# Cached keys turned in 32x32 blocks on VectorE, and logits on 32x32 TensorE tiles

## What is computed

```python
def moba_sample(q, k_new, v_new, cache_k, cache_v, page_table, slopes):
    ...
    k_past = cache_k[page_table].reshape(DB, past, H, D)
    ...
    k_mean = jnp.mean(kb.astype(jnp.float32), axis=2)
    ...
    idx, valid = moba_select(qh, q_pos, k_mean)
    ...
    o = moba_attend(qh, q_pos, k_sel, v_sel, idx, valid, k_own, v_own, ob * MOBA_BLOCK, slopes)

def trunk_layer(x, hist, start_pos, attend, norm1_g, w_in, w_pool, pool_scale, w_out, norm2_g, w_gate, w_up, w_down):
    h = rmsnorm(x, norm1_g)
    z = h @ w_in
    q, k, v, u = jnp.split(z, [ATTN_WIDTH, 2 * ATTN_WIDTH, 3 * ATTN_WIDTH], axis=-1)
    ...
    a = attend(q, k, v)
    p, new_hist = pool_mixer(u, hist, start_pos, w_pool, pool_scale)
    x = x + jnp.concatenate([a, p.astype(a.dtype)], axis=-1) @ w_out
    h2 = rmsnorm(x, norm2_g)
    x = x + (jax.nn.silu(h2 @ w_gate) * (h2 @ w_up)) @ w_down
```

## Time and profile before

| what | value |
|---|---|
| time, median of 3 runs | 1643.3 us (1643.12 to 1644.52) |
| the profiled execution | 1645.28 us |
| its span in the trace | 1643.3 us |
| PE busy | 1570.4 us, 96% |
| DVE, ACT, POOL busy | 759.0, 600.8, 104.1 us |
| read from HBM, mean rate | 328.10 MB, 203 GB/s |
| cached-attention phase | 81.5 to 581.5 us |

### The profile page before, as it was taken

How to read it: one execution, slowest core, us unless ns; L and a number is a source line. 1 busy time by engine, 2 the same in 40 slices (tenths; PEclk the granted TensorE clock), 3 DMA queues, 4 the chain that set the end, 5 groups by cost and what they waited for, 6 DMA issues and landing times.

```text
span 1643.3 us, 33559 instructions
## 1 busy us (share of the span) xinstructions
PE 1570.4 (96%) x12884; PEld 1400.6 (85%) x12884; DVE 759.0 (46%) x1202; ACT 600.8 (37%) x874; POOL 104.1 (6%) x184
## 2 busy tenths in 40 slices
PE   6999999999999978899999999999999999999987
PEld 5976676666666657799999999999999999999986
DVE  4533233133133133556555555454545555555545
ACT  4333233332333333335433333333333434333333
POOL 3004151000000010002000000000000000000003
PEclk9998999999999987999999999999999999999998
DMA  5667988989889744745545455555555454544531
GB/s 194 224 202 254 336 306 292 341 283 326 320 308 322 269 132 153 225 165 160 164 167 166 166 158 168 163 163 164 166 166 166 155 171 162 164 165 155 177 128 58
DMA packets 154368, 333.80 MB, mean 203 GB/s; under 512 B 10464, under 2 KB 44313, under 8 KB 153728
## 3 DMA queue, kind: packets, MB, share of 16 engines
q1 hardware_dynamic: 154311, 333.05, 60.4%
HBM read 328.10 MB, written 5.27 MB: 203 GB/s over the span
## 4 chain that ended last, share of the span: by engine, by line
PE 93%; DVE 3%; ACT 2%; issue 1%; DMA 1%; SPq 0%; POOL 0%; DVEq 0%; POOLq 0%; ACTq 0%
PE bank L1185 24%; PE bank L1187 23%; PE bank L1186 23%; PE bank L1191 10%; PE bank L1295 6%; PE bank L1267 4%; PE bank L1328 1%; ACT kT L483 1%; DMA vec<-in_pool_scale 1%; PE bank L1361 1%; PE bank L1434 0%; DVE w_lo L709 0%; DVE d L793 0%; PE bank L1421 0%; ACT px L609 0%
## 5 line engine op out<-in xcount | busy, mean ns | idle before, releaser
L1185 PE MATMUL bank<-hh,w_hi 128*128 128x288 f32 x2176 | 654.8, 301 | 11.7 <-DVE xT L886 6.6
L1186 PE MATMUL bank<-hl,w_hi 128*128 128x288 f32 x2176 | 644.0, 296 | 0.0
L1187 PE MATMUL bank<-hh,w_lo 128*128 128x288 f32 x2176 | 642.2, 295 | 0.0
L709 DVE TENSOR_TENSOR w_lo<-w_raw,w_hi 128x1024 fp32r<-128x1024 f32 (+1 forms) x376 | 443.3, 1184 | 406.9 <-ACT w_hi L483 403.8
L483 ACT ACTIVATE w_hi<-w_raw 128x1024 fp32r<-128x1024 f32 x312 | 328.3, 1058 | 510.9 <-PE bank L1187 508.8
L1185 PEld LDWEIGHTS bank<-hh,w_hi 128*128 128x128 f32 x2176 | 410.1, 188 | 27.2 <-issue 17.0
L1187 PEld LDWEIGHTS bank<-hh,w_lo 128*128 128x128 f32 x2176 | 411.7, 189 | 0.0
L1186 PEld LDWEIGHTS bank<-hl,w_hi 128*128 128x128 f32 x2176 | 410.9, 189 | 0.1
L483 ACT ACTIVATE kT<-bank 128x512 f32<-128x512 f32 x256 | 149.4, 597 | 278.6 <-PE bank L1191 278.3
L1185 PE MATMUL bank<-ah,w_hi 128*128 128x288 f32 x704 | 210.0, 298 | 9.5 <-DVE af L1041 5.4
L1187 PE MATMUL bank<-ah,w_lo 128*128 128x288 f32 x704 | 210.1, 298 | 0.0
(11 more groups left out here) (176 smaller groups left out, 679.6 us busy)
## 6 DMA issues: line engine op xcount, KB each, us to landing
kpage<-in_cache_k SPq DMA_DIRECT2D x128, 512.0 KB, 5.6
vpage<-in_cache_v SPq DMA_DIRECT2D x128, 512.0 KB, 5.0
w_raw<-in_w_gate SPq DMA_DIRECT2D x88, 512.0 KB, 3.5
w_raw<-in_w_up SPq DMA_DIRECT2D x88, 512.0 KB, 3.5
w_raw<-in_w_down SPq DMA_DIRECT2D x88, 512.0 KB, 3.5
w_raw<-in_w_in SPq DMA_DIRECT2D x64, 384.0 KB, 6.6
w_raw<-in_w_out SPq DMA_DIRECT2D x32, 512.0 KB, 4.8
w_raw<-in_w_in SPq DMA_DIRECT2D x16, 512.0 KB, 4.2
```

The lines of the kernel that those rows point to most:

```text
L709: V.tensor_tensor(w_lo[:, s, 0:width], w_raw[:, s, 0:width], w_hi[:, s, 0:width].bitcast(F32), ALU.subtract).then_inc(lo_ready, 1)
L1185: PE.matmul(o, wh, xh[:, c, :], start=start and i == 0, stop=False)
L1186: PE.matmul(o, wh, xl[:, c, :], start=False, stop=False)
L1187: last = PE.matmul(o, wl, xh[:, c, :], start=False, stop=stop and i == len(chunks) - 1)
```

## The change

K pages are no longer turned by PE. DVE turns each page in place, in blocks of 32x32 (`turn_k`, one 128x1024 instruction for a page, four for a quad). A logit is a sum over 4 blocks of 32 of the head's 128 dimensions. These four sums accumulate in PSUM, and the 32 keys in a block lie in the free dimension, so that a matmul has 32 rows (32 key rows of a page, after the turn 32 dimensions), 32 stationary columns and 256 moving columns (4 pages, 2 heads, 32 keys). The 16 matmuls for one block of 32 dimensions go to the 16 tiles of 32x32 of the array. Both heads of a pair have their queries in the stationary block, and the half that belongs to the other head is dropped later by `pick`. For this, q is replicated to all row groups once (`replicate_q`, 4 matmuls; `qrep`) and spread with zeros into `qr` for each sequence (`pad_q`). The logits lie in four banks (`S`, 2 to 5) in another order, so `scaled_logits` is one reduce over 1024 columns, eight operations of 128x128 and four small ones; before it was one operation and one reduce of 128x512, and a small one. The copies to `kT` on ACT are gone.

Weight tiles of this phase are 512x256 (24 matmuls, 48 tiles, 4 for each block of 256 columns, in two banks), all within the first six of the eight steps. ACT makes `w_hi` of them, and DVE computes `w_lo` in place of `w_raw`; raw slots are 6 instead of 4 and wait for `w_used` of the tile six before. K is loaded two quads ahead and waits for `qk_done` of the quad two before, the first two K quads wait for nothing, each K page has a semaphore of its own, and the order on SP in a quad is two tiles, K, V. The steps are written out, without the loop. The running maxima and sums of a sequence stay on all partitions (`ml_sp`) and are brought to 32 by one matmul after the last step.

```diff
-            def load_k(i, j, free=True):
-                if free:
-
-                    sp.wait_ge(kt_in, 32 * i + 8 * j - 8)
+            def load_k(i, j):
+                n = NQUADS * i + j
+                if n >= 2:
+
+                    sp.wait_ge(qk_done, n - 1)
                 for g in range(4):
...
+            load_k(0, 0)
+            load_k(0, 1)
+            for i in range(NB):
                 for j in range(NQUADS):
-                    for k in (2 * j, 2 * j + 1):
...
+                    if i < KVU_STEPS:
+                        load_kvu(8 * i + 2 * j)
+                        load_kvu(8 * i + 2 * j + 1)
+                    ahead = NQUADS * i + j + 2
+                    if ahead < NQUADS * NB:
+                        load_k(ahead // NQUADS, ahead % NQUADS)
+                    if i:
+                        load_v(i - 1, j)
...
             def load(t, src, free=True):
 
-                n, _, s = t
+                n, _, s, _ = t
                 if free:
-                    sp.wait_ge(lo_ready, n - 3)
+                    sp.wait_ge(w_used, n - RAW + 1)
...
+            def turn_k(i, j):
+                n = NQUADS * i + j
+                for g in range(4):
+                    dve.wait_ge(k_in[n % 2][g], 16 * (n // 2) + 16)
+                    V.transpose(kpage[:, n % 2, g, :], kpage[:, n % 2, g, :]).then_inc(k_turned, 1)
+
+            def scaled_logits(b):
+                dve.wait_ge(qk_done, NQUADS * b + NQUADS)
...
+                own.did(V.tensor_reduce(d4[:, :, :].rearrange("p a u -> p (a u)"),
+                                        S.rearrange("p a (s k) -> p s a k", s=4), AX.XY, ALU.add))
+                for e in range(2):
+                    for a in range(4):
+                        keys = slice(32 * a, 32 * a + 32)
+                        own.did(V.scalar_tensor_tensor(ss[:, :, keys],
+                                                       S[:, a, P * e:P * e + P].rearrange("p (n i) -> p n i", n=4),
+                                                       pick[:, e:e + 1], (past_bias, ss)[e][:, :, keys],
+                                                       ALU.mult, ALU.add))
...
+            pad_q(0)
+            turn_k(0, 0)
+            for i in range(NB):
+                lo_kvu(i, 0)
+                if i:
+                    select_blocks(i - 1)
+                    joint_max(i - 1)
+                turn_k(i, 1)
...
+                lo_kvu(i, 3)
+                if i < NB - 1:
+                    scaled_logits(i)
+                    pad_q(i + 1)
+                    turn_k(i + 1, 0)
...
-                def logits(j, h):
...
-                    for g in range(4):
-                        last = PE.matmul(S[32 * g:32 * g + 32, P * j:P * j + P], qz[:, 32 * h:32 * h + 32],
-                                         kT[:, h % 2, P * g:P * g + P], start=h == 0, stop=h == H - 1)
-                    last.then_inc(qk_done, 1)
...
+            def logits(b, j):
+                n = NQUADS * b + j
+                pe.wait_ge(k_turned, 4 * n + 4)
...
+                for c in range(4):
+                    for a in range(4):
+                        for x in range(4):
+                            at_ = STRIP * (4 * c + x) + PAD - j
+                            keys = kpage[32 * a:32 * a + 32, n % 2, :, :].rearrange(
+                                "p n (e x c i) -> p e x c n i", e=2, x=4, c=4)[:, :, x, c, :, :]
+                            last = PE.matmul(S[32 * x:32 * x + 32, a, :], qr[32 * a:32 * a + 32, at_:at_ + 32], keys,
+                                             start=j == 0 and c == 0, stop=j == NQUADS - 1 and c == 3)
+                last.then_inc(qk_done, 1)
...
+            replicate_q()
+            for i in range(NB):
+                logits(i, 0)
+                if i:
+                    block_sums(i - 1)
+                if i >= 2:
+                    combine(i - 2)
...
+                for j in range(1, NQUADS):
+                    logits(i, j)
+                    if i:
+                        values(i - 1, j - 1)
+                    if i < KVU_STEPS:
+                        kvu_tile(8 * i + 2 * j)
+                        kvu_tile(8 * i + 2 * j + 1)
+                if i:
+                    values(i - 1, NQUADS - 1)
```

More of the change, by code:

```diff
@@ L152, in step_program @@
         hl = sb("hl", [P, KC, T], F32R)
-        w_raw = sb("w_raw", [P, SLOTS, TE])
-        w_hi = sb("w_hi", [P, SLOTS, TE], F32R)
-        w_lo = sb("w_lo", [P, SLOTS, TE], F32R)
+        w_hi = sb("w_hi", [P, HI, TE], F32R)
+        raw = ExitStack()
+        w_raw = sb("w_raw", [P, RAW, TE], stack=raw)
+        raw.close()
+        w_lo = sb("w_lo", [P, RAW, TE], F32R)
         gains = sb("gains", [P, 56])
@@ L203, in step_program @@
         pre.close()
+        kv_a.close()
         post = ExitStack()
@@ L237, in step_program @@
         late.close()
[L239 to L242, removed]
+        banks = ctx.enter_context(nc.psum_tensor("banks", [P, 8, 512], F32))
+        bank = [banks[:, n, :] for n in range(8)]
+        WB = bank[0:2]
+        S = banks[:, 2:6, 0:2 * P]
         OB = bank[6:8]
@@ L400, in _, with load_v @@
[L400 to L407, removed]
+                    sp.dma_start(kpage[:, n % 2, g, :], page(ck, i, 4 * j + g)).then_inc(k_in[n % 2][g], 16)
+            def load_v(i, j):
+                n = NQUADS * i + j
+                if n:
+                    sp.wait_ge(v_done, n)
+                else:
+                    sp.wait_ge(xT_in, KC)
+                    sp.wait_ge(hist_T, 2)
+                for g in range(4):
+                    sp.dma_start(vpage[:, g, :], page(cv, i, 4 * j + g)).then_inc(v_in, 16)
@@ L798, in select_blocks @@
-            def select_blocks(i):
-                dve.wait_ge(bs_done, i)
+            own.did(V.tensor_scalar(pick[:, :], pair, SCALE, None, ALU.mult))
+            own.link(V.memset(qr[:, :], 0.0))
+            dve.wait_ge(sq_added, KC)
+            V.tensor_copy(rep_w, ident.rearrange("p (c i) -> p c i", c=4).unsqueeze(2).to_broadcast([P, 4, 4, 32])
+                          ).then_inc(rep_table, 1)
+            dve.wait_ge(rep_in, 1)
+            for x in range(2):
+                V.tensor_copy(qrep[:, 16 * x:16 * x + 16, :],
+                              OB[x].rearrange("p (s t) -> p s t", t=TS)).then_inc(rep_taken, 1)
@@ L988, in _ @@
             add_pool_half(15)
-            for k in range(2, SLOTS):
-                lo(tile_at(T_OA + k))
             dve.wait_ge(wo_taken, KC)
@@ L998, in add_group @@
                     ins.then_inc(quad_taken[quad], 1)
-            for k in range(4, 20):
+            for k in range(2, 20):
                 lo(tile_at(T_OA + k))
@@ L1182, in w_tile @@
                         a = width * i + P * m
[L1183 removed]
+                        wh, wl = w_hi[:, u, a:a + P], w_lo[:, s, a:a + P]
                         o = out[:, 0:T]
@@ L1383, in _ @@
             mixer(1)
-            p_turned(NB, True)
+            p_turned(NB - 1)
+            pe.wait_ge(l_saved, NB)
+            PE.matmul(OB[1][0:32, 16:32], tb("first"), ml_sp[:, :, :].rearrange("p a b -> p (a b)"), start=True,
+                      stop=True).then_inc(ml_in, 1)
             for r in range(2, 8):
```

466 lines of the change are left out of this document (219 added, 247 removed).

## The result

The changed kernel takes 1664.6 us (median of 4 runs, 1662.73 to 1665.54) against 1643.2 us for the kernel before: a ratio of 1.013, 95% interval 1.0113 to 1.0148. It is 21 us slower, where 1623 us, 20 us faster, was forecast.

The account below looks back on a forecast made before the run. PE was taken as the bound, transfers close behind. Start 11, step 0 48, steps 1 to 5 300, steps 6 and 7 110, clock 8: 477 against 500; +3 later, so 1623 us, own range 1600 to 1650, 8 in 10 1580 to 1690.

Parts of the forecast that it names:

- The price of the logits: PE, logits of a quad: 64 added matmuls with all 16 tiles overlapping, 2.0 us a quad.
- Rival 4: PE's logits: row tiles take turns, 6.9 us a quad, about 1672 us; chance 0.08.
- The turns: DVE, turning K pages: 128 turns of 128x1024 at 1.2 us each, 4.8 a quad.
- Rival 3: DVE's turns take two passes, 2.46 us each, about 1680 us; chance 0.13.
- I take 12.8: Steady quad with V and tiles: two loops and the transfers all sit at 12 to 13 us; 12.8 taken.
- The loop of the tiles: Steady quads: K and V issue, tile issue, landing, split, tiles and values to next logits but one, 26 us for two quads.
- the 8 us that were set aside for the clock: Whole phase: PE pauses more often and its clock falls in some steps, 8 us added.
- The border: Between sequences, steps 1 to 5: DVE work makes 16.6 instead of 12.8 us to next logits; +9 in all with thin queue.
- their 55 us: Steps 6 and 7, without tiles: 13 us a quad through the single V buffer, 3 at the border, 55 each.
- The start: From the z copies to the first logits: pick, table and q copies, PE 1.4, four turns, some 11 us.
- Rival 2: Phase's transfers thin throughout, slower than before, at 267 GB/s for over half the bytes: about 1665 us; chance 0.15.
- Rival 1: Phase's transfer queue never runs dry, 151 MB at 414 GB/s: about 1580 to 1600 us; chance 0.17.

Follow-up runs that it names:

- the mended order: Changed kernel with SP issuing the next quad's tiles, then V, then K: 1615.3 us; with the start filled and last values behind the next logits too, 1589.8 us.
- the junk: Junk matmuls on PE between logits and values in steps 6 and 7: ten in the changed kernel, 1665.1 us; eight in the fastest (1589.8 us), 1595.6 us.

## Why the prediction was wrong

The direction was wrong, and by the steps it was this:

- **What bounds before** was read rightly: PE. Its relief was real (112 us less busy time), and PE was indeed no longer last.
- **The price of the logits** was too low, 2.0 against 2.68 us. In the first pass the instructions of the 16 tiles start 7 ns apart, but a pass of the sixteen takes 0.335 us on average (2.68 over 8) instead of 0.215. By the Trainium skill, "TensorE: Matmul & The Clock Gate", Part 3, the estimate was 2.6, and the trace agrees with the page. On PE, which has slack, 0.7 us a quad matter little, but SP issues K pages only when the logits are done, so they lie on the loop below. Rival 4 (6.9) is excluded.
- **The turns** were right, 1.213 us. Rival 3 is excluded; the estimate of 2.5 us, from the Trainium skill's "VectorE: DVE Perf Modes", The three transpose paths, is twice what an fp32 page of 128x1024 takes, and the measurement decides. The four turns do stand right ahead of the logits of a sequence's second quad (13.4 us in most steps), but the run with quarter turns shows that shortening them moves the time to the quads behind.
- **The step that failed is "I take 12.8"** for a steady quad. The quads inside steps 1 to 5 took 14.4 us on average, which is 4.8 of the 5.5 us that a step took beyond the 60. The loop of the tiles, reckoned at 26 us for two quads, took 30.5 to 31.6. Its sum names the logits but has no term for them: they took 2.7. The values, 1.9 in the sum, aren't in series. Issue and landing were put at 15.6 us and took 17.5 in the quad of step 2: the landing of 6.6 us came from the kernel before, with tiles of 384 KB and a median of four transfers in flight at their issue; now it was 7.7 to 10.0 with five to seven in flight in the loops that were read. The two tiles took 8.1 us instead of 6.4, at the lower clock for part of the time. That last item is of the size of the 8 us that were set aside for the clock: 1.7 us in each such loop, and one of them stands in each of steps 2 to 5.
- **The border** of steps 1 to 5 was nearly right in size and wrong in mechanism. The forecast had 12.8 + 9 = 21.8 us for it and what follows from it; the border took 22.3 on average. But the 16.6 us to the next logits were put down to DVE's work (scaling, four turns, selection), and it is another path: two groups of values in a row on a single V buffer, with the next logits behind them. The order of PE shows this (L1316 x16 ahead of L1333 in the listing above), and I had reckoned only with DVE there. Moving the second group behind the logits cut it to 14 to 17. In steps 6 and 7 the size was wrong too: the border stands in their 55 us with 16, and took 21.9 from values to values, while V's loop took 13.0 to 14.5 a quad where 13 was taken.
- **The start** was 12.5 from the z copies instead of 11, since q's replication ran at the lower clock, 3.40 us where 1.4 was put for PE, after PE's pause.
- **Rival 2** was on the right side of zero with the wrong mechanism: the mean rate in the steps was 309 to 324 GB/s, as before, and the queue was thin because nothing had been issued. Rival 1, a full queue, held only in the mended order, and with 375 to 384 GB/s instead of its 414. By its own sum it would run from 1567 us, not from 1580. The 358 GB/s of the Trainium skill's "DMA: Bandwidth & Descriptors", Specifications, is passed there over 55 us windows, not only over 5.

So the gain went into a new wait. Before, PE's 60 us of work in a step of 63 covered nearly every landing; without it, the loops through SP show, and they were 65 us. Since the loops that were reckoned are near the time before (60 against 63 us a step), an error of 9% in a step turned the sign. What stays open is how much of the lower clock's cost could be had back, as the junk that raised it stood in the path itself.

## What to carry to other kernels

When an engine that bound is relieved, list for every queue that issues transfers what stands ahead of each one, and follow a loop from use to use with landing times for the place that it will have in that queue, not the one that it had. Write the engine's own work into the loop with its time; here the logits were named and not counted. More slots don't help a transfer that is issued behind one that waits: six raw slots were there, and PE still waited for tiles until they were moved ahead of the waiting K pages, worth 21 us alone and 49 with V. With a single buffer, look for two uses in a row on the consumer, for there its whole round trip shows. And read a test quad by quad before calling it without effect: the junk on PE gained in three quads what it lost in others.

## What the runs showed of the hardware

Sixteen 32x32 tiles of fp32 matmuls with 256 columns run in parallel, 128 instructions in 2.68 us, on row tiles as well as on column tiles. A transfer's landing time grew with what was in flight at its issue: in the changed kernel's phase tiles of 512 KB took a median of 7.5 us with four transfers in flight (4 tiles), 8.0 with five (20) and 9.2 with six (19). A turn of 128x1024 fp32 in 32x32 blocks takes 1.213 us, as long as an elementwise operation of that size (1.23). One core read 384 GB/s for 55 us. PE at the lower granted clock took 3.65 us for values that take 1.95 at the higher one.
